# Gate steps joined, four fill positions moved, the last token sums and the first loads regrouped in a three-branch encoder kernel

## The reference

```python
h = rmsnorm(x, norm_g)
(qa, ka, va, ga, qb, kb, vb, ab, gb, cq, ckv, kr, gc, mg) = split_cols(h @ w_in)
za = (swa_sink_attention(rope(qa), rope(ka), va, a_sinks) * silu(ga)) @ w_oa
log_a = log_sigmoid(ab @ w_alpha + b_alpha) / B_GATE_TAU
# GLA, per chunk of 64 frames: g = cumsum(log_a), k_dec = k * exp(g_end - g),
#   state = exp(g_end) * state + k_dec^T v, every frame of the chunk reads q @ state
zb = (rmsnorm(gla(qb, kb, vb, log_a), b_head_g) * silu(gb)) @ w_ob
zc = (mla(rmsnorm(cq) @ w_uq, rmsnorm(ckv) @ w_ukv, kr) * silu(gc)) @ w_oc
m = sigmoid(mg)
x = x + (m[0] * za + m[1] * zb + m[2] * zc) @ w_out
# after both layers: rmsnorm(x, final_g)
```

## Time and profile before

| | us |
|---|---|
| median of 3 runs (lowest to highest) | 984.53 (984.47 to 984.61) |
| the profiled execution | 984.31 |
| its span | 982.5 |
| TensorE busy | 967.0 (98%) |
| TensorE weight loads busy | 788.9 (80%) |
| VectorE busy | 577.9 (59%) |
| ScalarE busy | 403.5 (41%) |
| GpSimd busy | 1.6 |
| DMA, mean over the span | 93 GB/s |

### The profile page before, as it was taken

The page is one execution under the profiler, slowest core; times in us unless marked ns, Lnnn a source line. Parts: engine busy times, 40 slices in busy tenths (PEclk is TensorE's granted clock), DMA queues, the critical chain, the costliest instruction groups (busy, mean ns, idle before and its releaser), DMA issues.

```text
span 982.5 us, 13477 instructions
## 1 busy us (share of the span) xinstructions
PE 967.0 (98%) x5440; PEld 788.9 (80%) x5440; DVE 577.9 (59%) x943; ACT 403.5 (41%) x769; POOL 1.6 (0%) x6
## 2 busy tenths in 40 slices
PE   9999999999999999999999999999999999999996
PEld 7978878887888877788888888888878787777885
DVE  7846465347547565665556654744573566565844
ACT  6443343226533354532435323432463424554323
POOL 0000000000000000000000000000000000000000
PEclk9999999999999999999999999999999999999998
DMA  7324323321224212122323332223222332111212
GB/s 267 128 74 132 108 65 109 106 88 63 87 96 129 86 65 65 46 84 91 102 73 115 105 119 95 84 88 107 81 70 86 110 116 65 66 65 58 94 43 86
DMA packets 29808, 91.38 MB, mean 93 GB/s; under 512 B 4321, under 2 KB 6625, under 8 KB 29618
## 3 DMA queue, kind: packets, MB, share of 16 engines
q1 hardware_dynamic: 28914, 89.64, 28.2%
q10 hardware_dynamic: 832, 0.87, 0.3%
HBM read 84.67 MB, written 2.23 MB: 88 GB/s over the span
## 4 chain that ended last, share of the span: by engine, by line
PE 87%; ACT 5%; DVE 4%; issue 1%; DMA 1%; SPq 1%; POOLq 0%; POOL 0%; ACTq 0%; DVEq 0%
PE ring L581 70%; PE nat L581 7%; PE nat L780 3%; PE aux L822 2%; PE nat L787 2%; ACT work L1023 1%; ACT w_hi L838 1%; PE aux L808 1%; DMA raw<-pieces 1%; PE nat L794 1%; DVE work L1335 1%; DVE w_lo L1117 0%; SPq L448 0%; ACT gates L969 0%; PE nat L760 0%
## 5 line engine op out<-in xcount | busy, mean ns | idle before, releaser
L581 PE MATMUL ring<-act_hi,w_hi 128*128 128x512 f32 x832 | 331.1, 398 | 0.0
L581 PE MATMUL ring<-act_hi,w_lo 128*128 128x512 f32 x832 | 324.4, 390 | 0.0
L581 PE MATMUL ring<-act_lo,w_hi 128*128 128x512 f32 x832 | 324.2, 390 | 0.0
L838 ACT ACTIVATE w_hi<-raw 128x1024 fp32r<-128x1024 f32 x152 | 160.9, 1061 | 389.8 <-PE ring L581 358.0
L1117 DVE TENSOR_TENSOR w_lo<-raw,w_hi 128x1024 fp32r<-128x1024 f32 x152 | 185.4, 1221 | 53.4 <-ACT w_hi L838 53.3
L581 PEld LDWEIGHTS ring<-act_hi,w_hi 128*128 128x128 f32 x832 | 156.2, 188 | 37.0 <-issue 6.1
L581 PEld LDWEIGHTS ring<-act_hi,w_lo 128*128 128x128 f32 x832 | 156.1, 188 | 33.5
L581 PEld LDWEIGHTS ring<-act_lo,w_hi 128*128 128x128 f32 x832 | 156.3, 188 | 30.5
L1440 DVE SCALAR_TENSOR_TENSOR gates<-ring,rstd 128x512 f32<-128x512 f32 x72 | 49.7, 691 | 137.3 <-PE ring L581 137.3
L581 PE MATMUL ring<-y_hi,w_hi 128*128 128x512 f32 x192 | 74.7, 389 | 0.0
L581 PE MATMUL ring<-y_lo,w_hi 128*128 128x512 f32 x192 | 74.7, 389 | 0.0
(11 more groups left out here) (209 smaller groups left out, 1004.1 us busy)
## 6 DMA issues: line engine op xcount, KB each, us to landing
raw<-pieces SPq DMA_DIRECT2D x152, 512.0 KB, 3.5
xt<-x_t SPq DMA_DIRECT2D x8, 256.0 KB, 5.6
bank_a<-work SPq DMA_DIRECT2D x32, 64.0 KB, 2.0
out_t<-gates SPq DMA_DIRECT2D x7, 256.0 KB, 2.3
raw<-pieces SPq DMA_DIRECT2D x4, 256.0 KB, 5.3
rope<-tables SPq DMA_DIRECT2D x1, 1024.0 KB
bank_a<-work SPq DMA_DIRECT2D x32, 32.0 KB, 1.9
bank_g<-k_rope_dram SPq DMA_DIRECT2D x8, 64.0 KB, 3.2
```

The source lines that it names most:

```text
L581: mm = pe.matmul(dst, stationary, moving, start=start and i == 0, stop=stop and i == 2)
L838: nc.scalar.activation(w_hi[:, n % HL, :], raw[:, n % RAW, :], ACT.Copy).then_inc(hi_split.sem, 1)
```

## The change

- The first weight parts of pieces 0 and 1 are issued on ScalarE's queue: 256 columns of piece 0, the parameters, 512 columns of piece 1, the other 256 columns of piece 0. SP issues the rest as before, without these two.
- `gla_gate` and `gla_decay` become one step each, over all four frame tiles, in the upper halves of the four `nat` banks instead of `aux`. `gla_end` 0 multiplies `log_a` by a weight of 32 columns (`member`, of which two are not zero) into four groups of 32 partitions; ScalarE copies that, and `gla_end` 1 transposes it twice.
- `gla_turn` stands one quarter later, with the steps behind it. `turn_a` has three quarters ahead of it behind `divide_a`, not two. In the MLA loop the fifth step has one quarter fewer, the sixth one more.
- In the tail `token_sum(0)` stands behind k = 7 instead of k = 5, the first spread behind k = 2 instead of k = 4. The last squares are not added by VectorE: TensorE adds both parts in PSUM (`last_sum`), with two products into a free bank behind each. VectorE scales 7 tiles of the second half, GpSimd 1.

```diff
-    q = 4 * PQA[0]
-    step(("quarter", q), ("quarter", q + 1), ("quarter", q + 2), ("gla_gate", 1), ("quarter", q + 3))
-    q = 4 * PQA[1]
-    step(("quarter", q), ("quarter", q + 1), ("gla_decay", 0), ("quarter", q + 2), ("gla_decay", 1), ("k_dec", 0),
-         ("quarter", q + 3), ("gla_end", 0))
-    half(PQB[0], 0)
+    piece(PQA[0])
+    half(PQA[1], 0)
+    step(("gla_decay", 0), ("gla_end", 0), ("k_dec", 0))
+    half(PQA[1], 1)
+    step(("quarter", 4 * PQB[0]), ("gla_end", 1), ("quarter", 4 * PQB[0] + 1))
     step(("latent", 0))
     half(PQB[0], 1)
     half(PN2[0], 0)
...
-    step(("tanh", 4), ("gla_turn", 0))
+    step(("tanh", 4))
+    q = 4 * (m + 1)
+    step(("quarter", q), ("gla_turn", 0))
     for k in range(B_HEADS):
-        half(m + 1 + k // 2, k % 2)
-        if k % 2:
-            step(("tanh", 5 + k // 2))
+        for n in range(q + 1 + 2 * k, q + 3 + 2 * k):
+            step(("quarter", n))
+            if n % 4 == 3:
+                step(("tanh", 5 + k // 2))
         step(("gla_out", k), ("gla_hi", k))
         if k > 0:
...
+    step(("quarter", q + 9), ("gla_lo", B_HEADS - 1), ("quarter", q + 10), ("quarter", q + 11), ("tanh", 7))
...
-        quarters(2)
+        quarters(3)
...
-        quarters((1, 1, 2, 3)[qt])
+        quarters(3 if y > TT else 1)
...
-AUX = [s for s in SCHEDULE if s[0] in ("rms", "rstd_nat", "gla_gate", "gla_decay", "gla_end", "latent", "turn_ab")]
+AUX = [s for s in SCHEDULE if s[0] in ("rms", "rstd_nat", "gla_end", "latent", "turn_ab")]
...
-        later, member = con[:, LATER:LATER + P], con[:, MEMBER:MEMBER + 2]
+        later, member = con[:, LATER:LATER + P], con[:, MEMBER:MEMBER + 32]
...
+        nat_gate = quad[:, :, 256:512]
...
+        HEADS = ((0, slice(0, 256)), (1, slice(0, 512)), (0, slice(256, 512)))
...
+        DVE_TILES, HALF = 7, S // 2
...
-                if j < 2:
-                    sp.dma_start(raw[:, j, 0:512], pieces[j, :, 0:512]).then_inc(head_loaded[j].sem, 16)
-                elif j in (3, 4):
+                if j in (3, 4):
...
+                for lo, hi in ((0, 2), (2, 4), (4, 6), (6, KT if n == 0 else DVE_TILES)):
+                    sp.wait_ge(scaled.sem, KT * n + hi)
+                    sp.dma_start(out_t[:, lo:hi, hs], gates[:, lo:hi, hs]).then_inc(out_sent[0].sem, 16)
+            sp.wait_ge(out_sent[0].sem, 16 * 8)
...
-                        if (m, k) == (2, 5):
+                        if (m, k) == (2, 7):
                             pe.wait_ge(o_read.sem, o_read.at(DEPTH, 0))
                             token_sum(0)
-                        elif (m, k) == (3, 4):
+                        elif (m, k) == (3, 2):
...
-                token_sum(1)
+                last_sum()
...
+            def last_sum():
+
+                for squares, ready, n in ((sq_sum, half_acc, 3), (half_squares[:, 1, :], half_sq, 4)):
+                    pe.wait_ge(ready.sem, n)
+                    if n == 3:
+                        pe.wait_ge(picks_set.sem, 2)
+                    for t in range(2):
+                        mm = pe.matmul(aux[:, 4:8], squares[:, HALF + t * P:HALF + (t + 1) * P], picks[:, 2 - 2 * t:6 - 2 * t],
+                                       start=(n, t) == (3, 0), stop=(n, t) == (4, 1))
+                    if n == 4:
+                        mm.then_inc(token_sums.sem, 1)
+                    for _ in range(2):
+                        pe.matmul(nat[3][:, 0:256], ones, sq_sum[:, 0:256], start=True, stop=True)
...
+                        pe.wait_ge(ab_turned.sem, ab_turned.at(layer, 1))
+                        pe.wait_ge(v_a_set.sem, v_a_set.at(layer, TT))
+                        for t in range(TT):
+                            mm = pe.matmul(nat_gate[:, t, :], ab1[32:32 + B_RANK + 1, t * P:(t + 1) * P],
+                                           alpha_all[32:32 + B_RANK + 1, layer, :], start=True, stop=True)
+                        mm.then_inc(gate_in.sem, 1)
+                    elif name == "gla_decay":
+
+                        pe.wait_ge(gate_log.sem, gate_log.at(layer, 1))
+                        for t in range(TT):
+                            mm = pe.matmul(nat_gate[:, t, :], later, log_a[:, t, :], start=True, stop=True)
+                        mm.then_inc(decay_in.sem, 1)
+                    elif name == "gla_end":
+
                         aux_bank(layer, u)
...
+                        if i == 0:
                             for t in range(TT):
-                                mm = pe.matmul(aux[:, j * NC + 2 * t:j * NC + 2 * t + 2],
-                                               log_a[:, t, j * P:(j + 1) * P], member, start=True, stop=True)
+                                mm = pe.matmul(aux[32 * t:32 * t + 32, 0:256], member, log_a[:, t, :], start=True, stop=True)
+                        else:
+                            for j in range(2):
+                                mm = pe.transpose(aux[:, j * P:(j + 1) * P], totals[:, j * P:(j + 1) * P], ident)
...
-            act.dma_start(par_all[:, :, :], params).then_inc(par_loaded.sem, 16)
+            for n, (p, cols) in enumerate(HEADS):
+                act.dma_start(raw[:, p, cols], pieces[p, :, cols]).then_inc(head_loaded[n].sem, 16)
+                if n == 0:
+                    act.dma_start(par_all[:, :, :], params).then_inc(par_loaded.sem, 16)
...
+            head_hi_part(0)
...
                 if j == 1:
-                    act.wait_ge(head_loaded[1].sem, 16)
-                    nc.scalar.activation(w_hi[:, 1, 0:512], raw[:, 1, 0:512], ACT.Copy).then_inc(head_hi.sem, 1)
+                    head_hi_part(1)
+                    head_hi_part(2)
...
+                        act.wait_ge(gate_in.sem, gate_in.at(layer, 1))
+                        nc.scalar.activation(soft, nat_gate, ACT.Abs).then_inc(gla_soft.sem, 1)
+                        act.wait_ge(gla_soft.sem, gla_soft.at(layer, 1))
+                        nc.scalar.activation(soft, soft, ACT.Exp, scale=-1.0).then_inc(gla_soft.sem, 1)
+                        act.wait_ge(gla_soft.sem, gla_soft.at(layer, 2))
+                        nc.scalar.activation(soft, soft, ACT.Ln, bias=1.0).then_inc(gla_soft.sem, 1)
...
+                        act.wait_ge(decay_in.sem, decay_in.at(layer, 1))
+                        nc.scalar.activation(dec, nat_gate, ACT.Exp).then_inc(dec_set.sem, 1)
...
+                        if i == 0:
+                            nc.scalar.activation(totals, aux[:, 0:256], ACT.Copy).then_inc(aux_free.sem, 1)
+                        else:
+                            for j in range(2):
+                                one = nc.scalar.activation(decay[:, NC * j:NC * j + NC].rearrange("p (t c) -> p t c", t=TT),
+                                                           aux[:, j * P:(j + 1) * P].rearrange("p (t m) -> p t m", t=TT)[:, :, 0:2],
+                                                           ACT.Exp)
...
+                nc.vector.memset(picks, 0.0).then_inc(picks_set.sem, 1)
+                dve.wait_ge(picks_set.sem, 1)
+                nc.vector.memset(picks[:, 2:4], 1.0).then_inc(picks_set.sem, 1)
...
-                sum_half(3)
...
+                        dve.wait_ge(gla_soft.sem, gla_soft.at(layer, 3))
+                        nc.vector.scalar_tensor_tensor(log_a, nat_gate, 0.0, soft, ALU.min,
+                                                       ALU.subtract).then_inc(gate_log.sem, 1)
```

More of the change, by code:

```diff
@@ L178, in make_schedule @@
             step(("gla_lo", k - 1))
-    half(m + 3, 0)
-    step(("gla_lo", B_HEADS - 1))
-    half(m + 3, 1)
-    step(("tanh", 7))
+    step(("quarter", q + 9), ("gla_lo", B_HEADS - 1), ("quarter", q + 10), ("quarter", q + 11), ("tanh", 7))
     for j in range(4, 8):
@@ L354, in build_hybrid_trunk @@
         warm = merged[:, 7, :]
+        totals = work[:, 6, 0:256]
         o_nat = [work[:, b, :] for b in range(4)]
@@ L380, in build_hybrid_trunk @@
         x_loaded = [sig(f"x_loaded{i}", 0) for i in range(KT)]
-        head_loaded = [sig(f"head_loaded{p}", 0) for p in range(2)]
+        HEADS = ((0, slice(0, 256)), (1, slice(0, 512)), (0, slice(256, 512)))
+        head_loaded = [sig(f"head_loaded{n}", 0) for n in range(3)]
         head_hi, head_lo = sig("head_hi", 0), sig("head_lo", 0)
@@ L482, in _ @@
             for n, hs in enumerate(halves):
-                for j in range(0, KT if n == 0 else DVE_TILES, 2):
-                    sp.wait_ge(scaled.sem, KT * n + j + 2)
-                    sp.dma_start(out_t[:, j:j + 2, hs], gates[:, j:j + 2, hs]).then_inc(out_sent[0].sem, 16)
-            sp.wait_ge(out_sent[0].sem, 16 * 7)
+                for lo, hi in ((0, 2), (2, 4), (4, 6), (6, KT if n == 0 else DVE_TILES)):
+                    sp.wait_ge(scaled.sem, KT * n + hi)
+                    sp.dma_start(out_t[:, lo:hi, hs], gates[:, lo:hi, hs]).then_inc(out_sent[0].sem, 16)
+            sp.wait_ge(out_sent[0].sem, 16 * 8)
             sp.wait_ge(out_sent[1].sem, 16)
@@ L974, in _ @@
```

(22 more changed lines are left out.)

46 lines of the change are left out of this document (15 added, 31 removed).

## The result

| | before | after |
|---|---|---|
| median of 4 runs each, us (lowest to highest) | 984.50 (984.10 to 984.61) | **976.69** (976.39 to 976.97) |
| the profiled execution | 984.31 | 976.97 |
| its span | 982.5 | 975.2 |
| granted clock over the span | 0.996 | 0.999 |

The ratio is 0.9921, 95% interval [0.9904, 0.9939]. Forecast were 976.0 us and a range of 973.2 to 979.0. The two profiled spans differ by 7.3 us; the forecast's own sum was 8.5. So the time lies where it was expected, but one term went the other way. Here is where the 7.3 us came from, place by place.

The account below looks back on a forecast made before the run. TensorE, busy 98% of the span, was taken to bound the kernel; 0.3 + 2 x (0.4 + 0.8 + 0.8 + 0.3 + 0.6) + 2.4 = 8.5 us off 984.31 gave 975.8, 976.0 on the runs' median; range 973.2 to 979.0.

Parts of the forecast that it names:

- loads at the start: First weight loads on two queues: earlier landing lets TensorE start piece 3 earlier, 0.3 us saved, bounds nothing to 1.5.
- gate, a layer: GLA gate: one call of 8 passes in place of two of 4 saves one switch, 0.4 us a layer.
- totals, a layer: Chunk totals: four products in four column groups overlap, plus two transposes, instead of 8 small products; 0.8 us a layer saved.
- GLA turn, a layer: Transposes of the GLA heads: a quarter ahead removes idle time and restarted weight loads, 0.8 us a layer saved.
- window turn less the new wait, a layer: First window-attention turn: 1.0 us lost to divisions covered, new 0.7 us wait before second score; 0.3 a layer saved.
- MLA score, a layer: Sixth MLA score: its 0.55 us idle for ScalarE's copies goes, with the restart 0.6 us a layer saved.
- tail: Kernel's end: earlier scales and last sums, spread near full clock, last output issued earlier; 2.4 us saved, less 0.6 at half clock.
- a place not named: Sign of a wrong prediction: TensorE shows a wait of over 1 us somewhere the prediction did not name.
- Rival 2: Start: the two queues give nothing because the DMA engines are nearly full, other places pay as forecast; 976.3 us, chance 0.20.
- rival 1: Chunk totals: column groups do not overlap, or only in pairs, so the totals save nothing; 978.6 us, chance 0.15.
- Rival 3: Window attention: the new wait before the second score does not arise; 974.6 us, chance 0.10.
- Rival 4: Start: the longer stall before piece 3 lets TensorE's clock fall, making the kernel slower; 988.0 us, chance 0.02.

Follow-up runs that it names:

- experiments 1 and 2: The changed kernel with the old start, 976.42 us; and the kernel before with only the new start, 985.53 us, ratio 1.0008.
- Experiment 3: The changed kernel with only piece 1's first half issued on SP's queue again: 975.66 us.
- experiment 9: The changed kernel itself, unaltered, run once more: 976.83 us.
- Experiment 7: The changed kernel with the four chunk-total products all written to one column group instead of four: 979.17 us.
- Experiment 6: The changed kernel with one ScalarE tanh issued behind the first window turn's four copies instead of ahead of them: 975.42 us.
- experiment 8: The changed kernel without the four filler products beside the last token sums: 976.70 us.

## Why the prediction was right, and where it was not

The time came out 0.7 us above the forecast. The mechanism held at every place but one, the start, and of the tail's reasons one, the fillers, was not needed. By its own steps, between the two profiled spans:

| step | forecast, us | measured, us |
|---|---|---|
| loads at the start | 0.3 saved | 1.27 **lost** between the profiles; 0.3 to 0.9 lost by the runs of experiments 1 and 2 |
| gate, a layer | 0.4 | 2.67 - 2.12 = 0.55 |
| totals, a layer | 0.8 | 1.80 - 0.76 - 0.24 = 0.80 |
| GLA turn, a layer | 0.8 | 0.85 |
| window turn less the new wait, a layer | 1.0 - 0.7 | 0.98 - 0.65 |
| MLA score, a layer | 0.6 | 0.62 |
| tail | 2.4 | 2.1 |
| sum | 8.5 | -1.27 + 2 x 3.15 + 2.1 = 7.1 of 7.3 |

With the 0.3 to 0.9 lost at the start the sum is 7.5 to 8.1, and the medians differ by 7.8. That it came so near the forecast is in part luck: the start missed by 0.6 to 1.2 us and the tail by 0.3, and two layers of 3.15 instead of 2.9 gave 0.5 of it back.

- **The start failed, in sign.** I bounded it between 0 and 1.5 us gained, by the rate of the early stretch, and let no loss in: I compared the bytes ahead of *piece 2's* landing, which the change leaves the same. But the change also alters which transfer lands when. The half of piece 1 became the third on its queue, beside x's third tile on SP's, and it was the next thing that ScalarE had to split. It lands 1.35 us later, and then ScalarE stands for the quarter behind it too. Experiment 3 shows the place: with that transfer alone moved back the loss is gone, and by the medians the start is 0.8 better than the old one, which is inside my bounds. Why a third transfer on that queue takes so long (6.77 us from issue to landing) is not shown. The sentence "TensorE only waits longer before piece 3" was wrong too: the idle of 0.59 us there was gone, since TensorE itself came later; the landing that I had made the measure of the term moved as well, from 13.84 to 14.22, and nothing waited for it. A wait before piece 1 was in none of my terms or rivals: 0.78 us in the first profile of the change, 1.02 in the second (experiment 9), where I had set over 1 us in a place not named as a sign of being wrong.
- **Rival 2** named the right place and too small a price. The Trainium skill, "Trainium Kernel Development and Optimization", Key Constraints, says that the queues interleave on the same 16 DMA engines and that issuing from several saves issue time only. The trace of the change agrees on the rate, 277 beside 281 GB/s; the three kernels with only two quarters on that queue moved 300 to 309, which is more than that. The Trainium skill, "DMA: Bandwidth & Descriptors", Queues, rings and completion order, says besides that an engine takes its queues in turn, packet by packet; the landings of the change are such as this would give, the second transfers of both queues at 4.98 and 5.20, the third at 7.81 and 8.43, but no run tests it.
- **Gate and totals:** I took the price of both gate calls from the first (1.25); the second cost 1.41, so the gate gave 0.15 more. With the decay's 2 x 0.87 taken off, the totals' first step costs 2.50 - 1.74 = 0.76, where I took 0.8 between 0.5 and 2.1. Experiment 7 shows that the groups overlap, which was the open bound; rival 1 is out.
- **The window turn** went as written: the old wait gone, the new one at 0.58 where 0.7 was forecast, by the chain that was named (divisions, residual, gate, tanh, copies). Experiment 6 shows that this order, and not the copies' length, makes the wait. Rival 3 is out.
- **GLA and MLA:** the idles are gone, and the MLA turn just finds its operand: it starts 0.06 us behind the last division.
- **The tail** went by its steps; the spread is at the full clock. That the fillers "keep TensorE busy between" and so hold the clock is not what decides it (experiment 8): without them the idles are 0.84 and 1.01 us where they were 2.10 and 1.01, and the clock is full through the spreads. That the shorter idle is the reason is argued, not tested apart.
- **Rival 4** did not come: after the gap of 0.78 us the granted clock is 1.00 up to 973.4, behind the last product.

## What to carry to other kernels

A second issuing queue is first of all a second *order*: before a transfer is moved to it, list what lands when on both, and ask for each landing which in-order engine stands next to it. Here two short, first-needed parts stood well there, and a half behind the first, or two more quarters behind the two, arrived late. A fill quarter brings its helpers' work with it, so after moving one, look at what the copying engine now does ahead of the copies: moving that one step cost nothing and gave 1.3 to 1.4 us, where shifting the phase by a quarter lost 1.5. And a term of a few tenths read off two profiles at the start of a program needs several executions, since the landings there alone move by 0.7 us.

## What the runs showed that I had not expected

- The seven profiles with three weight transfers on ScalarE's queue moved 265 to 280 GB/s from 2 to 7 us, the one with four 283, the two with the old start 281 and 274, the three with two quarters on that queue 300 to 309. Why the last is faster was not tested.
- With the same 14 warming products TensorE's clock rose from half to full as early as 4.9 us and as late as 7.8 (the passes start 0.43 us apart up to there and 0.21 behind it). In the change's first profile it rose at 7.44, and the first product started 0.40 us behind the end of the residual that it needs (7.04), where the other profiles show 0.15, those with a late rise (7.23, 7.80) among them; the wait for piece 1 then hid this.
- Without fillers the clock stayed full through idles of 0.84 and 1.01 us and a few small products, and fell 1.1 us after the spreads began, when they were done; in the kernel before, idles of 2.10 and 1.01 us around four small products were followed by half the clock.
